# Modulation of an adaLN block gathered as rows: ScalarE scales its weights and makes its high sums, GpSimd only adds

## The reference, cut to what matters

```python
def swiglu_ffn(x, w_in, w_out):                 # w_in 1024 x 5632, w_out 2816 x 1024
    gate, up = jnp.split(x @ w_in, 2, axis=-1)
    return (jax.nn.silu(gate) * up) @ w_out
...
# first_block
h = h + 0.5 * swiglu_ffn(rmsnorm(h, ffn1_norm[layer]), ffn1_w_in[layer], ffn1_w_out[layer])
...                                             # mixer
h = h + 0.5 * swiglu_ffn(rmsnorm(h, ffn2_norm[layer]), ffn2_w_in[layer], ffn2_w_out[layer])
return rmsnorm(h, final_norm)
...
# second_block, x is the first block's result
c_act = jax.nn.silu(c)
mod = c_act @ w_ada[l] + b_ada[l]               # 1 x 1024 times 1024 x 6144
shift1, scale1, gate1, shift2, scale2, gate2 = [m[:, None, :] for m in jnp.split(mod, 6, axis=-1)]
h = rms_norm(x, g_pre_mix[l]) * (1.0 + scale1) + shift1
```

## Time and profile before

| | |
|---|---|
| median of 3 runs | 1006.28 us (1006.11 to 1006.47) |
| profiled execution | 1004.26 us |
| its span in the trace | 1002.4 us |
| granted TensorE clock over the span | 0.991 |
| busy: TensorE | 975.8 us, 97% |
| busy: VectorE | 779.9 us, 78% |
| busy: GpSimd | 511.0 us, 51% |
| busy: ScalarE | 501.8 us, 50% |
| a modulation step's multiply by c_act (L692), 24 of them | 90.6 us, 3775 ns each |

### The profile page before, as it was taken

The page is one execution under the profiler, slowest core; times in us unless marked ns, Lnnn a source line. Parts: engine busy times, 40 slices in busy tenths (PEclk is TensorE's granted clock), DMA queues, the critical chain, the costliest instruction groups (busy, mean ns, idle before and its releaser), DMA issues.

```text
span 1002.4 us, 18812 instructions
## 1 busy us (share of the span) xinstructions
PE 975.8 (97%) x7645; PEld 926.8 (92%) x7645; DVE 779.9 (78%) x810; ACT 501.8 (50%) x587; POOL 511.0 (51%) x302
## 2 busy tenths in 40 slices
PE   9999999999989999999999999999989989999997
PEld 8999999998979899999999999978979979999996
DVE  5776565799995679887787779998978887768764
ACT  7433433477541474434334756667657454343432
POOL 4575767610054037577577699999940104314400
PEclk9999999999998999999999999999989999999999
DMA  8966858747360277686776475572236517675641
GB/s 270 360 211 227 275 194 276 242 129 211 96 198 8 84 224 244 232 270 209 261 241 213 140 194 159 142 216 85 85 109 204 193 50 245 228 247 195 216 161 43
DMA packets 166494, 190.06 MB, mean 190 GB/s; under 512 B 10654, under 2 KB 155628, under 8 KB 166316
## 3 DMA queue, kind: packets, MB, share of 16 engines
q1 hardware_dynamic: 165580, 186.13, 57.1%
q0 software_dynamic: 688, 3.07, 1.1%
q10 hardware_dynamic: 176, 0.15, 0.1%
HBM read 187.17 MB, written 2.16 MB: 189 GB/s over the span
## 4 chain that ended last, share of the span: by engine, by line
PE 73%; DVE 15%; POOL 4%; issue 3%; ACT 2%; SPq 1%; DMA 1%; ACTq 0%; DVEq 0%; POOLq 0%
PE ps L2079 46%; PE ps L2123 11%; PE ps L2131 9%; DVE wl L1348 5%; DVE ps L1756 2%; POOL work L825 2%; POOL con L822 2%; PE ps L2364 1%; PE ps L2310 1%; ACT wh L856 1%; PE ps L2175 1%; SPq L564 1%; POOL work L818 1%; PE ps L2151 1%; PE ps L2235 1%
## 5 line engine op out<-in xcount | busy, mean ns | idle before, releaser
L2079 PE MATMUL ps<-xh,wh 128*128 128x256 f32 x1208 | 340.1, 282 | 6.4 <-DVE work L1375 3.2
L2079 PE MATMUL ps<-xl,wh 128*128 128x256 f32 x1208 | 335.4, 278 | 0.0
L2079 PE MATMUL ps<-xh,wl 128*128 128x256 f32 x1208 | 335.2, 278 | 0.0
L1353 DVE TENSOR_TENSOR wl<-raw,wh 128x2048 fp32r<-128x2048 f32 x78 | 231.5, 2968 | 67.4 <-ACT wh L862 67.1
L2079 PEld LDWEIGHTS ps<-xh,wh 128*128 128x128 f32 x1208 | 228.1, 189 | 12.3 <-issue 7.1
L2079 PEld LDWEIGHTS ps<-xl,wh 128*128 128x128 f32 x1208 | 227.8, 189 | 0.5
L2079 PEld LDWEIGHTS ps<-xh,wl 128*128 128x128 f32 x1208 | 227.5, 188 | 0.0
L862 ACT ACTIVATE wh<-raw 128x2048 fp32r<-128x2048 f32 x78 | 149.9, 1922 | 138.3 <-PE ps L2079 101.4
L1348 DVE TENSOR_TENSOR wl<-raw,wh 128x2048 fp32r<-128x2048 f32 (+1 forms) x72 | 181.5, 2527 | 32.7 <-ACT wh L856 32.0
L692 POOL TENSOR_TENSOR ada_raw<-ada_raw,c_act 128x2048 f32<-128x2048 f32 x24 | 90.6, 3775 | 206.5 <-DMA ada_raw<-in_w_ada 201.3
L856 ACT ACTIVATE wh<-raw 128x2048 fp32r<-128x2048 f32 (+1 forms) x74 | 139.5, 1889 | 59.4 <-PE ps L2079 42.3
(11 more groups left out here) (426 smaller groups left out, 1773.0 us busy)
## 6 DMA issues: line engine op xcount, KB each, us to landing
raw<-in_ffn_w_in SPq DMA_DIRECT2D x43, 1024.0 KB, 7.6
ada_raw<-in_w_ada SPq DMA_DIRECT2D x24, 1024.0 KB, 5.1
raw<-in_ffn_w_out SPq DMA_DIRECT2D x22, 1024.0 KB, 6.5
raw<-in_w_in SPq DMA_DIRECT2D x18, 1024.0 KB, 5.3
raw<-in_w_mlp_in SPq DMA_DIRECT2D x16, 1024.0 KB, 5.5
raw<-in_w_mlp_out SPq DMA_DIRECT2D x16, 1024.0 KB, 4.9
raw<-in_w_mix_in SPq DMA_DIRECT2D x14, 1024.0 KB, 5.4
raw<-in_w_mix_out SPq DMA_DIRECT2D x4, 1024.0 KB, 5.2
```

The costliest lines, as they stand in the source:

```text
L1353: dve.tensor_tensor(wl[:, s % SLOTS, :], raw[:, s % SLOTS, :], wh[:, s % SLOTS, :].bitcast(F32), ALU.subtract).then_inc(low_done, 1)
L2079: mm = pe.matmul(bank[:, m * T:(m + 1) * T], w[:, k, m * P:(m + 1) * P], r[:, k, :], start=(m == 0 and k == 0 and j == 0), stop=(k == KT - ...
```

## The change

The 20 early steps of the modulation take another way; the four late ones stay as they were.

- ScalarE multiplies by `c_act`: `scale_rows`, eight copies of 128 x 256 with a scale per partition, in place in `ada_raw`. They stand behind copy two of a pass, ahead of the rounded hidden values and copy three, and scale the step after the present one. Only steps 0 and 10 are still multiplied by GpSimd.
- GpSimd makes the three sums, now into a tile of their own (`ada_fold`), and as a fourth operation the low part of the sum (sum minus its rounded copy).
- ScalarE makes the rounded copy, `high_sum`, right ahead of `scale_rows`: a copy of 128 x 20 that picks the step's place in a row of zeros with a one, and the copy of 128 x 256.
- TensorE adds up the partitions with a single matmul of 512 columns (256 high and 256 low) whose 20 weight columns hold a one in the step's place: a step fills one row of `ps[7]`. The two matmuls of one column and the zeros over the gate bank are gone from the pass.
- After bank 2 of ffn2's last deep slab TensorE turns the rows back into columns (`turn_rows`, four matmuls of 20 columns); ahead of that VectorE copies the rows out of the bank, and the bias add waits for the turn.
- SyncE's load of a step waits for the first sum of the step before (`ada_part`), since only that reads `ada_raw`, and no longer for the last.
- GpSimd's three other places: a memset of the convolution's padding moves behind ffn1's loop, the last part of the constant table and a blank tile are sent after step 0, whose last operation now waits for ScalarE, and the angles of the rope wait for step 20.

```diff
@@ SyncE
-            def modulation(step):
+            def modulation(step, late=False):
-                if not isinstance(step, int) or step:
+                if late:
                     sp.wait_ge(*at("ada_free", step))
+                elif not isinstance(step, int) or step:
+                    sp.wait_ge(*at("ada_part", step * 5 - 3))
                 sp.dma_start(ada_raw[:, :, :], rows["w_ada_2"][:, :, bass.ds(step * 256, 256)]).then_inc(S("ada_loaded"), 16)
...
@@ GpSimd
+            def modulation(step, name, scale=True):
+                flat = ada_raw[:, :, :].rearrange("p k m -> p (k m)")
+                fold, parts = ada_fold[name], ada_parts[name]
+                if scale:
+                    pool.wait_ge(*at("ada_loaded", step * 16 + 16))
+                    pool.tensor_tensor(ada_raw[:, :, :], ada_raw[:, :, :], c_act[:, :].unsqueeze(2).to_broadcast([P, KT, 256]),
+                                       ALU.mult).then_inc(S("ada_part"), 1)
+                else:
+                    pool.wait_ge(*at("ada_free", step))
+                pool.wait_ge(*at("ada_part", step * 5 + 1))
+                pool.tensor_tensor(fold[:, :], flat[:, 0:1024], flat[:, 1024:2048], ALU.add).then_inc(S("ada_part"), 1)
+                pool.wait_ge(*at("ada_part", step * 5 + 2))
+                pool.tensor_tensor(fold[:, 0:512], fold[:, 0:512], fold[:, 512:1024], ALU.add).then_inc(S("ada_part"), 1)
+                pool.wait_ge(*at("ada_part", step * 5 + 3))
+                pool.tensor_tensor(fold[:, 0:256], fold[:, 0:256], fold[:, 256:512], ALU.add).then_inc(S("ada_part"), 1)
+                pool.wait_ge(*at("ada_part", step * 5 + 5))
+                pool.tensor_tensor(parts[:, 1, :], fold[:, 0:256], parts[:, 0, :].bitcast(F32), ALU.subtract)\
+                    .then_inc(S("ada_free"), 1)
...
             with pool.Fori(0, FF_STEPS - 2) as i:
-                modulation(i + 1)
+                modulation(i + 1, "ffn1", scale=False)
...
@@ ScalarE
+                def high_sum(step):
+                    if not isinstance(step, int) or step:
+                        act.wait_ge(*at("ada_taken", step))
+                    act.wait_ge(*at("ada_part", step * 5 + 4))
+                    act.activation(step_pick[:, :], step_line[:, bass.ds(step * -1 + (ADA_EARLY - 1), ADA_EARLY)], ACT.Copy)
+                    act.activation(ada_parts[name][:, 0, :], ada_fold[name][:, 0:256], ACT.Copy).then_inc(S("ada_part"), 1)
+                def scale_rows(step):
+                    act.wait_ge(*at("ada_loaded", step * 16 + 16))
+                    for k in range(KT):
+                        ins = act.activation(ada_raw[:, k, :], ada_raw[:, k, :], ACT.Copy, scale=c_act[:, k:k + 1])
+                    ins.then_inc(S("ada_part"), 1)
...
                     cast_in_loop(s + 4, i, 3, 1)
+                    high_sum(i + first)
+                    scale_rows(i + (first + 1))
                     act.wait_ge(taken, i * 3 + (s + 3))
                     round_hidden(i + 2)
                     cast_in_loop(s + 5, i, 3, 1)
...
                 silu(FF_STEPS)
+                high_sum(first + FF_STEPS - 2)
                 round_hidden(FF_STEPS, last_high[name])
...
@@ VectorE
                 dve.wait_ge(*at("ada_taken", ADA_EARLY))
+                dve.tensor_copy(ada_rows, ps[7][0:ADA_EARLY, :]).then_inc(S("ada_rows"), 1)
+                dve.wait_ge(*at("ada_cols", 1))
...
@@ TensorE
+            def modulate(step, name):
+                pe.wait_ge(*at("ada_free", step + 1))
+                pe.matmul(ps[7][0:ADA_EARLY, :], step_pick[:, :], ada_parts[name].rearrange("p a t -> p (a t)"), start=False, stop=False, skip_group_check=True)\
+                    .then_inc(S("ada_taken"), 1)
...
+            def turn_rows():
+                pe.wait_ge(*at("ada_rows", 1))
+                for half in range(2):
+                    for part in range(2):
+                        mm = pe.matmul(ps[7][:, half * ADA_EARLY:(half + 1) * ADA_EARLY],
+                                       ada_rows[:, part * T + half * P:part * T + (half + 1) * P], ident[0:ADA_EARLY, 0:ADA_EARLY],
+                                       start=(half == 0 and part == 0), stop=(part == 1), skip_group_check=True)
+                mm.then_inc(S("ada_cols"), 1)
...
                     deep(i * 3 + (s + 2), slab=s + 2, begin=begin)
-                    modulate(i + (0 if name == "ffn1" else FF_STEPS - 1))
-                    pe.wait_ge(*at(name + "_gate", i + 2))
-                    long_zeros(gate_bank)
+                    modulate(i + (0 if name == "ffn1" else FF_STEPS - 1), name)
...
                     if m in (1, 3, 5):
                         mm.then_inc(S(name + "_bank"), 1)
+                    if name == "ffn2" and m == 3:
+                        turn_rows()
```

More of the change, by code:

```diff
@@ L447, in two_blocks @@
         y_eps, z_eps, scale_m = kr, kr_raw, ps[6][:, T:2 * T]
+        ada_fold = {"ffn1": at_mat, "ffn2": w_v[:, 0:1024]}
+        ada_parts = {"ffn1": yl[:, 0:2, :], "ffn2": xh[:, 4:6, :]}
+        ada_rows = w_kn[0:ADA_EARLY, 0:512]
         gate_row, z_rows, z_junk = w_qn[:, 0:D], w_kn, w_v
@@ L663, in _ @@
                     deep(s + 1 + i * 6, s + 1, "w_mlp_out_2", i * 3 + r)
-                modulation(i + ADA_EARLY)
+                modulation(i + ADA_EARLY, late=True)
             for k in range(ADA_MLP * SLOTS + 1, MLP_STEPS):
@@ L684, in _, with modulation_late @@
             pool.memset(zero[:, :], 0.0).then_inc(S("zero"), 1)
-            pool.memset(qkvp[:, :, 0:3], 0.0).then_inc(S("pads"), 1)
+            ps_(pool.memset(step_line[:, :], 0.0))
+            ps_.sync()
+            pool.memset(step_line[:, ADA_EARLY - 1:ADA_EARLY], 1.0).then_inc(S("pads"), 1)
             pool.memset(mpad[:, :, 0:2], 0.0).then_inc(S("pads"), 1)
-            def modulation(step):
+            def modulation(step, name, scale=True):
[16 more added lines that the diff above has]
+                    .then_inc(S("ada_free"), 1)
+            def modulation_late(step):
                 flat = ada_raw[:, :, :].rearrange("p k m -> p (k m)")
@@ L693, in modulation @@
                                    ALU.mult).then_inc(S("ada_part"), 1)
-                pool.wait_ge(*at("ada_part", step * 3 + 1))
+                pool.wait_ge(*at("ada_part", step * 3 + 1 + 2 * ADA_EARLY))
                 pool.tensor_tensor(flat[:, 0:1024], flat[:, 0:1024], flat[:, 1024:2048], ALU.add).then_inc(S("ada_part"), 1)
-                pool.wait_ge(*at("ada_part", step * 3 + 2))
+                pool.wait_ge(*at("ada_part", step * 3 + 2 + 2 * ADA_EARLY))
                 pool.tensor_tensor(flat[:, 0:512], flat[:, 0:512], flat[:, 512:1024], ALU.add).then_inc(S("ada_part"), 1)
-                pool.wait_ge(*at("ada_part", step * 3 + 3))
-                if not isinstance(step, int) or step:
-                    pool.wait_ge(*at("ada_taken", step))
+                pool.wait_ge(*at("ada_part", step * 3 + 3 + 2 * ADA_EARLY))
+                pool.wait_ge(*at("ada_taken", step))
                 pool.tensor_tensor(ada_sum[:, :], flat[:, 0:256], flat[:, 256:512], ALU.add).then_inc(S("ada_free"), 1)
@@ L716, in _ @@
             pool.wait_ge(low_done, 3)
-            modulation(0)
+            modulation(0, "ffn1")
             pool.dma_start(con[:, N_CONST_FIRST:N_CONST], a["table"][:, N_CONST_FIRST:]).then_inc(S("con_rest"), 16)
@@ L783, in _ @@
             pool.memset(upad[:, :, 0:PAD], 0.0).then_inc(S("upads"), 1)
-            with pool.Fori(0, FF_STEPS - 1) as i:
-                modulation(i + (FF_STEPS - 1))
+            modulation(FF_STEPS - 1, "ffn2")
+            with pool.Fori(0, FF_STEPS - 2) as i:
+                modulation(i + FF_STEPS, "ffn2", scale=False)
+            pool.wait_ge(*at("ada_free", ADA_EARLY))
             pool.wait_ge(*at("pos_loaded", 16))
@@ L840, in _ @@
             with pool.Fori(0, ADA_MLP) as i:
-                modulation(i + ADA_EARLY)
+                modulation_late(i + ADA_EARLY)
         @block.scalar
@@ L895, in round_hidden @@
                     act.activation(high[:, :, :], pair(hid[:, 3, :]), ACT.Copy).then_inc(S(name + "_fh"), 1)
+                def high_sum(step):
[9 more added lines that the diff above has]
+                    ins.then_inc(S("ada_part"), 1)
+                first = 0 if name == "ffn1" else FF_STEPS - 1
                 cast(s0 + 3)
@@ L900, in ffn, with one_pass @@
                 round_hidden(1)
-                with act.Fori(0, FF_STEPS - 2) as i:
+                def one_pass(i):
                     s = s0 + 2
@@ L909, in ffn @@
                     cast_in_loop(s + 5, i, 3, 1)
+                with act.Fori(0, FF_STEPS - 2) as i:
+                    one_pass(i)
                 s = s0 + 3 * FF_STEPS - 4
@@ L2169, in one, with modulate_late @@
                 return k + 1
[L2171 removed]
+            def modulate(step, name):
+                pe.wait_ge(*at("ada_free", step + 1))
```

(3 more changed lines are left out.)

18 lines of the change are left out of this document (13 added, 5 removed).

## The result

The changed kernel is slower: 1011.25 us in the median of 14 runs (1006.64 to 1014.68) against 1006.05 (1003.28 to 1010.28) in the same number of runs of the kernel before, a ratio of 1.0049 with an interval of 1.0034 to 1.0063. The forecast was 1003.6, with a range of 998 to 1011.

The account below looks back on a forecast made before the run. TensorE, busy 97% of the span, was taken to bound the kernel. Ffn1 -3.0, ffn2 -2.4, first passes -0.8 and seams +3.5 gave -2.7: 1001.6 against the profiled 1004.26, 1003.6 as median, range 998 to 1011.

Parts of the forecast that it names:

- the ring through ScalarE's scaling: Feed-forward loops: first sum to low half 6.31, SyncE 0.16, loads 7.65, scaling 3.37; 17.5 us a turn, chance 0.56.
- third rival: Loops: another wait eats TensorE's shorter pass, so only first passes and seams count; +2.7, 1009 us, chance 0.08.
- The loads, 7.65: Loops: deep slab and modulation load together in 7.65 us, taken from one measured pair; range from 5.1 to 7.65.
- the 17.67 at which the sum changed sign: Length in us of a turn through ScalarE's scaling at which the forecast change in time is zero; +2.0 at 17.79.
- second rival: ScalarE's scaling copies don't overlap: scaling 4.06, turn 18.2 us, +9.7, 1016 us; chance 0.18 for longer copies or loads.
- Ffn1's slack, 2.7: Ffn1's loop: 2.7 us of slack before the turn through the scaling binds, 4.4 less 1.7 for a late start.
- Ffn2, -2.4: Ffn2's nine loop passes: 150.9 of TensorE plus 1.4 lost to the turn through the scaling, against 154.7; -2.4 us.
- The first passes, -0.8: The pass ahead of each feed-forward loop: each saves 0.4 us, together 0.8.
- The seam, +3.0: Ffn2's end: turning the rows within the last slab starts the residual 2.9 to 4.1 us later; 3.0 taken, bounds +0.4 to +4.1.
- M: Start of ffn2's last slab, 548.96 us in the earlier trace; there the first addition to the residual ran at M + 1.75.
- TensorE's own pass, 16.77: Feed-forward loops: a pass of TensorE alone, slabs 16.54 plus one 512-column matmul 0.23, takes 16.77 us; nine take 150.9.
- At nothing: Remaining zeros, moved table, blank tile, padding and angles were counted as costing nothing; uncovered, each under 1 us.

## Why the prediction was wrong

The mechanism was the one forecast: the ring through ScalarE's scaling, its links, their order and ScalarE's wait for the load. TensorE's wait was put at the wrong place: ahead of the deep slab for the low half (in the loops VectorE's L1405), where it was 0.1 at most, in place of the pass's end, where GpSimd's low part held it; the forecast named this as a sign of its third rival, but the experiments show the wait to follow from the ring. Wrong were sizes, in a sum that gives 1.6 us for each 0.1 us of ring.

- **The loads, 7.65.** This is the step that failed first. They took 8.18 us in the turn shown, and from the deep slab's issue to the scaling's start 7.9 to 8.3 in all 15 pairs of the two loops behind ffn1's first. The forecast took one measured pair and let the range end there, with 5.1 below it and nothing above. Why the pair takes longer is not shown; it does so in passes too in which the ring doesn't bind yet (8.00 and 7.92 in the first of ffn2). The other terms held: scaling 3.31 (3.37 forecast), to the low half 6.36 (6.31), SyncE 0.18 (0.16), the row matmul 0.23. The ring was 17.9 on average in place of 17.5, beyond the 17.67 at which the sum changed sign; by the forecast's own steepness that is +3.7, 1010. It is the second rival's outcome, by longer loads and not by copies that don't overlap.
- **Ffn1's slack, 2.7.** It was used up in one pass. The first pair there was issued at 34.99, 0.76 later than in the earlier trace rows, and landed 9.25 us after; why is not shown, and in two other runs with the same ring the same pair took 8.25 and 8.13. Ffn1 was to lose 3.1 to the ring and lost 8.5 (159.41 - 150.9).

```profile
34.99 0.37 SPq L546 DMA_DIRECT2D raw<-in_ffn_w_out  x1
...
44.24 3.31 ACT L939 ACTIVATE ada_raw<-ada_raw,c_act 128x256 f32<-128x256 f32 x8 [3.63 <-DMA ada_raw<-in_w_ada]
```

- **Ffn2, -2.4.** It was +1.4. The free passes were there, 16.57, 16.65, 16.68, as forecast; a slow one (17.29), four of 17.9 to 18.1 and a last of 16.90 followed.
- **The first passes, -0.8.** Together they gave nothing: ffn2's was 0.5 shorter, and ffn1's as well, but that began 1.0 late behind an early load (26.53 in place of 25.50).
- **The seam, +3.0.** 3.8, inside its outer bound. The first addition came at M + 6.4, 4.7 later than before, where 2.9 to 4.1 was forecast. The turn was worth 1.5 of the seam; the larger share is VectorE's last low half, 3.5 us behind M instead of 1, which the forecast let cost 1.2 at most.
- **TensorE's own pass, 16.77.** It is 16.56 at the fast pace and 17.2 at the slow one; that there are two was not in the sum.
- **At nothing.** The moved table, padding and angles show no wait in the profile after, and the zeros that remain once lie ahead of a wait of 1.7 us for that early load.

The balance in the profiled pair: +0.5 at the first loop, +2.4 in ffn1, -3.0 in the mixer, of which the clock gave 3.2 on the products shown, -0.5 and +1.4 in ffn2, +3.8 at the seam, +0.45 behind it; together 5.0 of 5.1. As the mixer's part goes with the clock and not with the change, the 5.2 of the medians is not split by these numbers to better than about 3 us.

## What to carry to other kernels

Work that waits for a transfer should not stand in an in-order queue ahead of work that releases that transfer: here one moved line made 11 us. When a forecast ring is within a few per cent of the bound it replaces, its largest term decides, and a range that ends at the one pair measured has no room for a longer one. The wait that the profile shows at the bounding engine can be the late end of a ring that runs elsewhere: cutting that wait alone moved it and saved nothing, so test a cut of each suspect.

## What the runs showed of the hardware that was not expected

Back-to-back matmuls of 256 columns run at one of two paces at a granted clock of 1.00: 48 in 5.44 or in 5.65 us, 0.113 or 0.118 each. In these traces the gate and up slab of a pass share one pace, the deep slab behind them mostly has it too, and one pace held for a whole loop, but for at most one pass, where zeros ended the passes. Over 18 passes this is up to 11 us, twice the effect of the change, so a part of each kernel's spread may be its paces, and some 3 us of it the clock in the mixer; no run separates that. What selects the pace is not shown.

A subtraction of 256 columns on GpSimd took 0.74 us in step 0, where it began ahead of a low half on VectorE, and 2.43 to 2.64 in the loops, where it began behind one. The Trainium skill, page "SBUF — State Buffer", section "🔬 SBUF: two separate sides", has GpSimd and VectorE take a shared pair of ports by an exclusive lock; the trace agrees as far as these durations and the earlier trace rows go. The same page's summary estimates transfers at about 358 GB/s; the two loads of 1.05 MB in 8.18 us came to 256 GB/s here, and all transfers of that window together to 296.
